# Expert inputs of a mixture-of-experts stage: rows scattered once to DRAM in slot order instead of gathered for every job

## The chip, the cores and the metric

The kernel runs on one core of one Trainium2 chip. The core has TensorE (PE for matmuls, PEld for its weight loads), VectorE (DVE), ScalarE (ACT), GpSimd (POOL) and SyncE (SP), and 16 DMA engines that all queues share. The metric is the device time of one execution in microseconds; less is better.

## The reference, cut to what matters

A two-layer decoder trunk on 256 tokens of width 1024, all in float32. Layer 0 is sparse attention and a dense SwiGLU of width 2816, layer 1 is stick-breaking attention and a top-2-of-8 expert SwiGLU. What the change touches is the last part:

```python
def moe_ffn(u, router_w, w_gate_up, w_down):
    logits = (tok @ router_w)
    top_vals, top_idx = lax.top_k(logits, 2)
    gates = jax.nn.softmax(top_vals, axis=-1)
    ...
    for e in range(8):
        y = y + dense_gates[:, e:e + 1] * swiglu(tok, w_gate_up[e], w_down[e])
```

The weights of the eight experts are 8 x (1024 x 5632 + 2816 x 1024) floats, and each is read from DRAM once.

## The kernel before, in words

The kernel is one hand-ordered program with one instruction stream for each engine and semaphores between them. Its stages are: attention of layer 0 (to about 104 us of the span), dense SwiGLU in 11 steps (about 17 us each in the middle, to 297 us), shared keys and values and layer 1's attention (to about 398 us), router and routing (to about 423 us), and then the experts.

**Jobs.** An expert gets its tokens in jobs of 96 slots. There are at least 8 jobs, one for each expert; experts with more than 96 tokens would get further ones, up to 24. Jobs 0 to 7 ran here. A job has 12 up tiles (`expert_up`, two transfers each, 2 MB a tile for the first eight and 1.5 MB for the last four) and 11 down tiles (`expert_dn`, 1 MB each). PE's order is written out in `iteration(k, i)`: up tile `i`, then down tile `i - 4`; up tiles 0 to 2 of the next job are put among the last down tiles of this one. Up tiles lie in a ring of 6, down tiles in a ring of 4, and SP refills a place in this fixed order as soon as PE has done with it. SP's transfers go through one queue (q1), those of POOL through another (q0).

**The input of a job** is `m_u`, the 96 tokens' rows transposed to 8 blocks of 128 x 96. Job 0 gets it from products of `h` with a 0/1 matrix `m_pick` on PE (`gather_first`). For job k + 1, during job k:

- DVE makes `m_pick` of the next job (`pick`, at i = 3).
- PE multiplies it with the token numbers (`slot_tokens`, at i = 5: 12 small matmuls with one column), and DVE turns the result into `slot_token`, 96 row numbers (`tokens_known`, at i = 6). A slot without a token gets row number 0.
- POOL fetches these 96 rows of `u_rows` by an indirect DMA into `m_x`, 96 partitions x 1024 (`fetch` in `save`). `u_rows` is the normalised stream, 256 x 1024, which POOL wrote to DRAM in `late_routing`'s time with two plain DMAs.
- PE transposes `m_x` in 8 pieces (`gather`, at i = 8), and DVE multiplies them with the norm's weight into `m_u` (`gathered`, at i = 9). ACT copies `m_u` to `m_u_now` between two jobs.

**The output of a job**, `m_y`, is saved by POOL to `y_rows`, a DRAM tensor of 24 x 96 rows of which rows from job 7 on are cleared beforehand: in attention of layer 0, by one DMA from a zeroed tile. After the last save, each token's two rows are gathered from `y_rows` with four indirect DMAs (`y_first`, `y_second`) while the last job runs, and the last job's own rows are added by products on PE.

**The dense stage** matters because of the clearing. Step i needs up tile i (2 MB, in runs of 1 KB) and down tile i (1 MB, in runs of 4 KB) from SP's queue. SP issues up tile i once DVE has split up tile i - 4, and right behind it down tile i - 2 once down tile i - 6 is split. ACT starts the split of a tile (`up_piece`, `dn_piece`), so an ACT row tells when a tile has to be there.

Of the kernel before, what the change touches and what calls it, by code (L numbers as in the profile page):

```python
# [44 lines left out]
NO_SLOT = -1.0e4  # L45
# [3 lines left out]
K_EPS, K_ROW, K_TOKEN = 928, 929, 945  # L49
# [7 lines left out]
T_IN, T_OUT, T_DENSE = 0, 5, 7  # L57
# [9 lines left out]
def program(nc, x, a_norm_w, a_w_in, a_q_norm_w, a_k_norm_w, a_w_out, kv_norm_w, kv_w, b_norm_w,  # L67
# [6 lines left out]
    with ctx:  # L74
        def sb(name, shape, dt=f32):
            return ctx.enter_context(nc.sbuf_tensor(name, shape, dt))

        def sem(name):
            return ctx.enter_context(nc.semaphore(name))
# [45 lines left out]
        slot_token = sb("slot_token", [SLOTS, 1], i32)  # L125
        u_rows = nc.dram_tensor("u_rows", (TOK, DM), f32, kind="Internal").ap()
# [81 lines left out]
        m_x = u[0:SLOTS, 0, :]  # L208
# [62 lines left out]
        u_ready, u_out, m_x_in, e_token_ps, e_token = (sem(n) for n in ("u_ready", "u_out", "m_x_in", "e_token_ps", "e_token"))  # L271
# [226 lines left out]
        def _(pe):  # L498
# [409 lines left out]
            def slot_tokens(j):  # L908

                pe.wait_ge(e_pick, j + 1)  # L910
                for t in range(NT):
                    for n in range(3):
                        mm = on_third(bank[4][THIRD * n:THIRD * n + THIRD, 0:1], m_pick[:, t, THIRD * n:THIRD * n + THIRD],
                                      cst[:, K_TOKEN + t:K_TOKEN + t + 1], n, t == 0, t == NT - 1)
                mm.then_inc(e_token_ps, 1)

# [10 lines left out]

            def gather(j):

                pe.wait_ge(m_x_in, 16 * j)  # L930
                for b in range(KD):
                    c = SLOTS * (b % 4)
                    mm = pe.transpose(bank[4 + b // 4][:, c:c + SLOTS], m_x[:, P * b:P * b + P], ident[0:SLOTS, 0:SLOTS])  # L933
                mm.then_inc(e_gather, 1)
# [79 lines left out]
            def iteration(k, i, last=False):  # L1014
                if i < E_UP or not last:
                    expert_up(k, i)
                if i == 5 and not last:
                    pe.wait_ge(e_u, k + 1)
                    slot_tokens(k + 1)
                if i == 8 and not last:  # L1020
                    gather(k + 1)
                if i == 6 and last:
                    pe.wait_ge(e_pick, k + 1)
                    pe.wait_ge(e_u, k + 1)
# [403 lines left out]
        def _(pool):  # L1428
# [4 lines left out]
            for j, (angle, first) in enumerate(((cos, 0), (sin, 16), (cos, 16), (sin, 0))):  # L1433
# [5 lines left out]
            pool.dma_start(y_rows[(NEXP - 1) * SLOTS:, :].rearrange("(j s) c -> s j c", s=SLOTS),  # L1439
                           m_y.unsqueeze(1).to_broadcast([SLOTS, JOBS - NEXP + 1, DM])).then_inc(y_cleared, 16)  # L1440
# [21 lines left out]
            for t in range(NT):  # L1462
                pool.wait_ge(u_ready, t + 1)
                pool.dma_start(u_rows[P * t:P * t + P, :], u[:, t, :]).then_inc(u_out, 16)
# [5 lines left out]
            pool.wait_ge(u_out, 16 * NT)  # L1470
# [14 lines left out]
            first_row, second_row, gate1, gate2 = (folded(v) for v in (first_row, second_row, gate1, gate2))  # L1485
# [9 lines left out]

            def save(k):

                pool.wait_ge(y_saved, k + 1)
                pool.wait_ge(e_gather, k + 1)
                pool.wait_ge(e_token, k + 1)  # L1500
# [16 lines left out]
            pool.wait_ge(e_gather, last_job + 1)  # L1517
# [13 lines left out]
        def _(dve):  # L1531
# [290 lines left out]
            dve.wait_ge(y_cleared, 16)  # L1822
            scaled_heads(q_T[:, 0:4, :], pair[bq_pair[0]]).then_inc(bq_sb, 1)
# [84 lines left out]
            def tokens_known(j):  # L1908
                dve.wait_ge(e_token_ps, j)
                dve.tensor_copy(slot_token[:, 0:1], bank[4][0:SLOTS, 0:1]).then_inc(e_token, 1)  # L1910

# [24 lines left out]
            def gathered(k):  # L1936
                dve.wait_ge(e_gather, k + 1)
                dve.wait_ge(e_u_now, k)
                w = nw[:, KD * NORM_F1:KD * (NORM_F1 + 1)].rearrange("p (b j) -> p b j", b=2).unsqueeze(3)\
                    .to_broadcast([P, 2, 4, SLOTS])  # L1940
                src = pair[2][:, :].rearrange("p (b c) -> p b c", b=2)[:, :, 0:4 * SLOTS].rearrange("p b (j c) -> p b j c", j=4)
                dve.tensor_tensor(m_u.rearrange("p (b j c) -> p b j c", b=2, j=4), src, w, ALU.mult).then_inc(e_u, 1)
# [29 lines left out]
            def iteration(k, i, last=False):  # L1972
                if i % 4 == 3 and i < E_UP:
                    hidden_step(k, i // 4)
                if i == STEPS - 1 + E_DN_LATE:
                    result(k)
                if i == 3 and not last:
                    dve.wait_ge(e_gather, k + 1)
                    pick(k + 1)
                if i == 6 and not last:  # L1980
                    tokens_known(k + 1)
# [11 lines left out]
            def late_routing():  # L1993
                for t in range(NT):
                    dve.tensor_scalar(u[:, t, :], h[:, t, :], rs[:, 3, t:t + 1], None, ALU.mult).then_inc(u_ready, 1)
# [3 lines left out]
                for t in range(NT):  # L1999
                    dve.tensor_tensor_scan(rows_f[:, 1, t, :], ones[:, 0:NEXP], routed[:, t, :], 0.0, ALU.mult, ALU.add)  # L2000
# [63 lines left out]
```

## Time and profile before

| what | value |
| --- | --- |
| median of 3 runs | 1129.88 us (1128.78 to 1129.98) |
| the profiled execution | 1128.54 us, its span 1126.7 us |
| granted clock of TensorE | 1.0 |
| PE busy | 1113.7 us, 99% of the span |
| DMA moved | 361.30 MB, mean 321 GB/s |
| one job (up tile 8 to up tile 8) | 86.5 us |

In the 40 slices of the span PE is busy in all of them. The DMA row has gaps up to the 14th slice and is at 9 tenths from then until the last two; the rate is near 411 GB/s in most of those slices.

### The profile page before, as it was taken

How to read it: one execution, taken by the hardware profiler on the slowest of the kernel's cores; microseconds unless marked ns; L12 is line 12 of the kernel's file. 1: busy time of each engine (PE TensorE's matmuls, PEld its weight loads, DVE VectorE, ACT ScalarE, POOL GpSimd, SP SyncE). 2: the span in 40 equal slices, each digit the busy share in tenths (PEclk: the TensorE clock that was granted, in tenths of full speed). 3: DMA queues.
4: the chain of work that ended last, by engine and by line, in shares of the span. 5: the costliest groups of instructions: out<-in, count | busy, mean ns of one | idle time of the engine just before them, and what ended most of it. 6: DMA issues, size and time to landing. Idle time of an engine off the chain costs nothing.

```text
span 1126.7 us, 32768 instructions
## 1 busy us (share of the span) xinstructions
PE 1113.7 (99%) x15160; PEld 893.7 (79%) x15160; DVE 304.8 (27%) x466; ACT 254.9 (23%) x384; POOL 30.5 (3%) x84
## 2 busy tenths in 40 slices
PE   9999999999999999999999999999999999999998
PEld 7768999999899876678778778778778778878765
DVE  3785645545664342001001010010010010110021
ACT  4775534434547531000000000000001000000000
POOL 0000000000000002000000000000000000000100
PEclk9999999999999999999999999999999999999999
DMA  9639976454144289999999999999999999999983
GB/s 337 214 126 295 335 272 214 160 187 150 57 168 150 75 346 399 363 412 409 397 411 411 396 411 411 392 411 410 398 411 411 383 411 410 385 411 391 410 357 128
DMA packets 114214, 361.30 MB, mean 321 GB/s; under 512 B 6872, under 2 KB 33920, under 8 KB 102816
## 3 DMA queue, kind: packets, MB, share of 16 engines
q1 hardware_dynamic: 109776, 343.78, 79.0%
q0 software_dynamic: 4080, 15.34, 4.0%
q8 instruction: 121, 1.98, 0.7%
q10 hardware_dynamic: 224, 0.09, 0.0%
q14 instruction: 13, 0.11, 0.0%
HBM read 347.65 MB, written 11.53 MB: 319 GB/s over the span
## 4 chain that ended last, share of the span: by engine, by line
PE 91%; DMA 4%; DVE 2%; ACT 1%; SPq 0%; issue 0%; ACTq 0%; DVEq 0%
PE pair L938 57%; PE pair L519 9%; PE pair L520 9%; PE pair L521 9%; DMA dn_ring<-in_moe_w_down 4%; PE pair L555 1%; PE pair L581 1%; PE pair L933 1%; PE pair L536 0%; DVE up_lo L1566 0%; PE pair L620 0%; DVE dn_ring L1671 0%; PE pair L923 0%; ACT up_hi L1075 0%; PE pair L857 0%
## 5 line engine op out<-in xcount | busy, mean ns | idle before, releaser
L938 PE MATMUL pair<-up_ring,work 128*32 128x256 f32 (+1 forms) x6144 | 323.9, 366 | 0.0
L938 PEld LDWEIGHTS pair<-up_ring,work 128*32 128x32 f32 x6144 | 239.0, 110 | 73.6
L938 PE MATMUL pair<-dn_ring,e_mem 128*32 128x256 f32 (+1 forms) x3168 | 245.7, 450 | 1.9 <-DMA dn_ring<-in_moe_w_down 1.7
L938 PEld LDWEIGHTS pair<-dn_ring,e_mem 128*32 128x32 f32 x3168 | 147.6, 110 | 76.9 <-DMA dn_ring<-in_moe_w_down 3.5
L938 PE MATMUL pair<-up_more,work 128*32 128x192 f32 (+1 forms) x3072 | 152.5, 352 | 0.0
L938 PEld LDWEIGHTS pair<-up_more,work 128*32 128x32 f32 x3072 | 133.2, 110 | 13.8
L519 PE MATMUL pair<-uT_hi,up_hi 128*128 128x256 f32 x480 | 135.5, 282 | 0.8 <-DVE uT_lo L1580 0.6
L1566 DVE TENSOR_TENSOR up_lo<-up_ring,up_hi 128x2048 fp32r<-128x2048 f32 x46 | 105.3, 2291 | 112.4 <-ACT up_hi L1075 112.3
L520 PE MATMUL pair<-uT_lo,up_hi 128*128 128x256 f32 x480 | 134.8, 281 | 0.0
L521 PE MATMUL pair<-uT_hi,up_lo 128*128 128x256 f32 x480 | 134.8, 281 | 0.0
L1390 ACT ACTIVATE e_mem<-pair 128x768 f32<-128x768 f32 (+1 forms) x24 | 18.2, 758 | 479.3 <-PE pair L938 479.3
L1961 DVE TENSOR_TENSOR e_mem<-e_mem,pair 128x768 f32<-128x768 f32 (+1 forms) x24 | 21.3, 888 | 333.9 <-PE pair L938 333.9
L1075 ACT ACTIVATE up_hi<-up_ring 128x2048 fp32r<-128x2048 f32 x46 | 87.9, 1913 | 101.5 <-PE pair L521 97.0
L519 PEld LDWEIGHTS pair<-uT_hi,up_hi 128*128 128x128 f32 x480 | 90.4, 188 | 2.1 <-issue 1.3
L520 PEld LDWEIGHTS pair<-uT_lo,up_hi 128*128 128x128 f32 x480 | 90.4, 188 | 0.4
L521 PEld LDWEIGHTS pair<-uT_hi,up_lo 128*128 128x128 f32 x480 | 90.4, 188 | 0.0
L519 PE MATMUL pair<-up_hi,uT_hi 128*128 128x512 f32 x128 | 51.7, 404 | 1.1 <-DVE uT_lo L1590 1.1
L1969 DVE COPY q_T<-pair 96x256 f32<-96x256 f32 x8 | 3.4, 420 | 179.2 <-PE pair L938 179.2
L520 PE MATMUL pair<-up_lo,uT_hi 128*128 128x512 f32 x128 | 50.6, 395 | 0.0
L521 PE MATMUL pair<-up_hi,uT_lo 128*128 128x512 f32 x128 | 50.5, 395 | 0.0
L1075 ACT ACTIVATE q_T<-pair 32x256 f32<-32x256 f32 (+2 forms) x30 | 14.3, 480 | 90.7 <-PE pair L938 82.1
L520 PE MATMUL pair<-dn_lo,hid_hi 128*128 128x512 f32 x80 | 31.6, 395 | 0.0
(299 smaller groups left out, 778.0 us busy)
## 6 DMA issues: line engine op xcount, KB each, us to landing
up_ring<-in_moe_w_gate_up SPq DMA_DIRECT2D x96, 1024.0 KB, 10.3
dn_ring<-in_moe_w_down SPq DMA_DIRECT2D x88, 1024.0 KB, 16.8
up_more<-in_moe_w_gate_up SPq DMA_DIRECT2D x32, 1024.0 KB, 12.9
up_ring<-in_moe_w_gate_up SPq DMA_DIRECT2D x32, 768.0 KB, 10.8
up_more<-in_moe_w_gate_up SPq DMA_DIRECT2D x32, 768.0 KB, 10.6
up_ring<-in_dense_w_gate_up SPq DMA_DIRECT2D x22, 1024.0 KB, 9.0
dn_ring<-in_dense_w_down SPq DMA_DIRECT2D x11, 1024.0 KB, 11.1
up_ring<-in_kv_w SPq DMA_DIRECT2D x4, 2048.0 KB, 7.9
```

What stands on the lines that cost most here:

```text
L519: pe.matmul(ps, a_hi, b_hi, start=start, stop=False, skip_group_check=shared)
L520: pe.matmul(ps, a_hi, b_lo, start=False, stop=False, skip_group_check=shared)
L521: return pe.matmul(ps, a_lo, b_hi, start=False, stop=stop, skip_group_check=shared)
L555: mm = pe.matmul(bank[2 * t + g][:, 0:I_HALF], uT_in[:, k, P * t:P * t + P], index_tile(half)[:, j, I_HALF * g:I_HALF * g + I_HALF], start ...
L581: mm = pe.matmul(bank[(NT * j + t) % 4][:, 0:cols], uT_in[:, k, P * t:P * t + P], up_tile(j, cols)[:, k, :], start=(k == 0), stop=(k == KD ...
L933: mm = pe.transpose(bank[4 + b // 4][:, c:c + SLOTS], m_x[:, P * b:P * b + P], ident[0:SLOTS, 0:SLOTS])
L938: return pe.matmul(out, a, w, start=start, stop=stop, tile_position=(0, THIRD * place), skip_group_check=True)
L1075: return act.activation(out_, in_, ACT.Copy, scale=scale)
L1390: act.activation(m_hid[:, 0:3 * cols].rearrange("p (n c) -> p n c", n=3), gate_ps[:, 0:768].rearrange("p (n c) -> p n c", n=3)[:, :, 0:col ...
L1566: dve.tensor_tensor(buffer(up_lo, n, 2048), raw_piece(n), buffer(up_hi, n, 2048).bitcast(f32), ALU.subtract).then_inc(up_l, 1 + unsplit)
L1961: dve.tensor_tensor(v, v, up_ps[:, 0:768].rearrange("p (n c) -> p n c", n=3)[:, :, 0:cols], ALU.mult).then_inc(e_raw, 1)
L1969: dve.tensor_copy(m_y[:, 512:768], bank[3][0:SLOTS, 0:256])
```

## The change

`u_rows` goes. In its place stands `x_rows`, 24 x 96 rows in slot order, of which the rows of jobs 1 to 23 are cleared with two DMAs. The clearing of `y_rows` moves from the first attention into the dense stage, in front of them. Once the slot rows are computed, POOL scatters the 256 rows of `u` into `x_rows` with four indirect DMAs (first choice and second choice of each token). In the jobs a fetch is four plain DMAs of 32 partitions x 3 x 256, whose place depends on the job number alone. `u` is written with its columns permuted so that 32 x 32 blocks come together, DVE transposes the fetched tile (128 x 768) by blocks into `m_xT`, and `gathered` reads that. `slot_tokens`, `gather`, `tokens_known` and the `pick` of jobs 1 to 6 go. DVE waits for the clearing before it reuses `q_T`.

```diff
+        rows_x = sb("rows_x", [P, 2, NT], i32)
+        x_rows = nc.dram_tensor("x_rows", (JOBS * SLOTS, DM), f32, kind="Internal").ap()
...
-        m_x = u[0:SLOTS, 0, :]
+        m_x = u[:, 0, 0:768]
+        m_xT = e_mem[:, 768 + GROUPS * 768:2 * 768 + GROUPS * 768]
...
-                if i == 5 and not last:
-                    pe.wait_ge(e_u, k + 1)
-                    slot_tokens(k + 1)
-                if i == 8 and not last:
-                    gather(k + 1)
...
+            pool.wait_ge(up_used, 2 * (T_DENSE + 3))
+            def clear(rows, first, end, done):
+                pool.dma_start(rows[first * SLOTS:end * SLOTS, :].rearrange("(j s) c -> s j c", s=SLOTS),
+                               m_y.unsqueeze(1).to_broadcast([SLOTS, end - first, DM])).then_inc(done, 16)
+            clear(y_rows, NEXP - 1, JOBS, y_cleared)
+            clear(x_rows, 1, 12, x_cleared)
+            clear(x_rows, 12, JOBS, x_cleared)
...
             def fetch(j):
-                pool.indirect_dma_start(m_x, None, u_rows, bass.IndirectOffsetOnAxis(slot_token[:, 0:1], 0)).then_inc(m_x_in, 16)
+                for place in range(4):
+                    part = slice(THIRD * place, THIRD * place + THIRD)
+                    src = x_rows[bass.ds(j * SLOTS, SLOTS), 256 * place:256 * place + 256]
+                    pool.dma_start(m_x[part, :].rearrange("t (n c) -> t n c", n=3),
+                                   src.rearrange("(n t) c -> t n c", n=3)).then_inc(m_x_in, 16)
...
+            pool.wait_ge(u_ready, NT)
+            pool.wait_ge(x_cleared, 32)
+            for which in range(2):
+                for t in range(NT):
+                    pool.indirect_dma_start(x_rows, bass.IndirectOffsetOnAxis(rows_x[:, which, t:t + 1], 0), u[:, t, :], None)\
+                        .then_inc(x_out, 16)
...
             def gathered(k):
-                dve.wait_ge(e_gather, k + 1)
+                dve.wait_ge(m_x_in, 64 * k)
+                dve.transpose(m_xT.rearrange("p (b t) -> p b t", t=THIRD), m_x.rearrange("p (b c) -> p b c", c=THIRD))\
+                   .then_inc(x_free, 1)
```

## Rows read from the trace of the kernel before

**Rows 1.** The page's slices: busy tenths, then GB/s of all DMA queues together.

```profile
PE   9999999999999999999999999999999999999998
DMA  9639976454144289999999999999999999999983
GB/s 337 214 126 295 335 272 214 160 187 150 57 168 150 75 346 399 363 412 409 397 411 411 396 411 411 392 411 410 398 411 411 383 411 410 385 411 391 410 357 128
```

**Rows 2.** Waits of PE: line waited for, us in total, times, longest.

```profile
PE pair L938 <- DMA dn_ring<-in_moe_w_down: 1.7, 1, 1.7
```

**Rows 3.** Windows: us, PE, PEld, DVE, ACT, POOL busy (instructions); PEclk, DMA share, GB/s.

```profile
452.00:538.00 86.00, 86.00 (x1567) 65.18 (x1563) 7.69 (x12) 4.67 (x8) 2.01 (x4) 1.00 1.01 398
...
971.00:1037.00 66.00, 66.00 (x1220) 49.17 (x1213) 4.62 (x6) 3.12 (x4) 1.14 (x2) 1.00 1.00 393
```

**Rows 4.** DMA issues in 480:509, 683:712, 1000:1029: xcount, KB, median us to landing.

```profile
dn_ring<-in_moe_w_down SPq DMA_DIRECT2D x3, 1024.0 KB, 10.8
...
dn_ring<-in_moe_w_down SPq DMA_DIRECT2D x4, 1024.0 KB, 15.3
...
dn_ring<-in_moe_w_down SPq DMA_DIRECT2D x3, 1024.0 KB, 21.5
```

**Rows 5.** Chain that ended last, its end: start, us, what.

```profile
1065.55 22.12 DMA dn_ring<-in_moe_w_down
...
1087.71 30.08 PE pair L938 x456
```

**Rows 6.** Timeline of PE in job 2: start, us, instructions; slot products, then transposes.

```profile
630.31 0.27 PE L938 MATMUL pair<-cst,work 128*32 128x1 f32 x11
...
652.55 0.88 PE L933 MATMUL pair<-cst,u 96*128 96x96 f32 x8
```

**Rows 7.** Windows of 6 us: at `u_rows`' write, a save, three fetches, `y_first`'s gather.

```profile
428.00:434.00 6.00, 6.00 (x116) 3.66 (x112) 0.00 (x0) 0.00 (x0) 0.00 (x0) 1.00 1.02 404
...
532.00:538.00 6.00, 6.00 (x107) 5.32 (x103) 1.44 (x4) 0.00 (x0) 0.18 (x1) 1.00 1.03 413
...
635.00:641.00 6.00, 6.00 (x106) 3.60 (x102) 0.00 (x0) 0.00 (x0) 0.00 (x0) 1.00 1.03 349
...
463.00:469.00 6.00, 6.00 (x107) 3.61 (x100) 0.00 (x0) 0.00 (x0) 0.00 (x0) 1.00 1.03 338
...
808.00:814.00 6.00, 6.00 (x108) 3.62 (x104) 0.00 (x0) 0.00 (x0) 0.00 (x0) 1.00 1.03 357
...
1061.00:1067.00 6.00, 5.95 (x104) 3.53 (x97) 0.00 (x0) 0.81 (x1) 0.00 (x0) 1.00 1.04 413
```

**Rows 8.** DMA in 120:150, the dense loads alone.

```profile
DMA packets 7781, 10.23 MB, mean 341 GB/s; under 512 B 152, under 2 KB 7003, under 8 KB 7778
```

**Rows 9.** Timeline of POOL: end of job 0's save; timeline of DVE: second hidden step, job 1.

```profile
535.74 0.18 POOL L1508 TENSOR_TENSOR tick<-tick 1x1 f32<-1x1 f32 x1 [7.09 <-DMA y_rows<-q_T]
...
560.71 0.98 DVE L1963 STREAM_TRANSPOSE e_mem<-e_mem 128x768 f32<-128x768 f32 x1
```

**Rows 10.** DMA issues in 60:120, then the queues in 96:102 (packets, MB, share).

```profile
y_rows<-q_T POOLq DMA_DIRECT2D x1, 6528.0 KB, 33.5
...
q0 software_dynamic: 400, 1.63, 86.6%
q1 hardware_dynamic: 301, 0.31, 14.4%
```

**Rows 11.** Timelines of SP and ACT in the dense stage, from 149 us.

```profile
154.02 0.99 SPq L423 DMA_DIRECT2D up_ring<-in_dense_w_gate_up  x2
...
170.98 0.99 SPq L423 DMA_DIRECT2D up_ring<-in_dense_w_gate_up  x2
...
149.75 1.92 ACT L1075 ACTIVATE up_hi<-up_ring 128x2048 fp32r<-128x2048 f32 x1 [3.71 <-PE pair L521]
...
206.04 1.04 ACT L1075 ACTIVATE dn_hi<-dn_ring 128x1024 fp32r<-128x1024 f32 x1
...
223.00 1.05 ACT L1075 ACTIVATE dn_hi<-dn_ring 128x1024 fp32r<-128x1024 f32 x1
```

More of the change, by code:

```diff
@@ L270, in program @@
         row_step = sem("row_step")
-        u_ready, u_out, m_x_in, e_token_ps, e_token = (sem(n) for n in ("u_ready", "u_out", "m_x_in", "e_token_ps", "e_token"))
+        u_ready, x_cleared, x_out, m_x_in, x_free = (sem(n) for n in ("u_ready", "x_cleared", "x_out", "m_x_in", "x_free"))
         block = ctx.enter_context(nc.Block())
@@ L905, in _ @@
             keep_clock(1)
[L908 to L915, printed above, removed]
             def gather_first():
@@ L926, in gather_first @@
                         mm.then_inc(first_gather if k < KD - 1 else e_gather, 1)
[L928 to L934, printed above, removed]
             def on_third(out, a, w, place, start, stop):
@@ L1484, in _ @@
             then_next(pool.tensor_tensor(gate2, gate, second, ALU.mult))
-            first_row, second_row, gate1, gate2 = (folded(v) for v in (first_row, second_row, gate1, gate2))
+            first_row, second_row = (folded(v) for v in (first_row, second_row))
+            then_next(pool.tensor_scalar(rows_x[:, 0, :].unsqueeze(2), first_row, NO_SLOT, None, ALU.add))
+            then_next(pool.tensor_scalar(rows_x[:, 1, :].unsqueeze(2), second_row, NO_SLOT, None, ALU.add))
+            pool.wait_ge(u_ready, NT)
[4 more added lines that the diff above has]
+                        .then_inc(x_out, 16)
+            gate1, gate2 = (folded(v) for v in (gate1, gate2))
             then_next(pool.tensor_scalar(spare[:, 0, 0:1], misc[:, 0, 6:7], float(SLOTS), float((NEXP - 1) * SLOTS) - NO_SLOT,
@@ L1494, in _ @@
             then_next(pool.tensor_scalar(rows_i[:, 1, :].unsqueeze(2), second_row, NO_SLOT, None, ALU.add))
+            pool.wait_ge(x_out, 16 * 2 * NT)
             def save(k):
                 pool.wait_ge(y_saved, k + 1)
-                pool.wait_ge(e_gather, k + 1)
-                pool.wait_ge(e_token, k + 1)
+                pool.wait_ge(x_free, k + 1)
                 pool.tensor_tensor(tick, tick, tick, ALU.mult).then_inc(tick_done, 1)
@@ L1516, in _ @@
             pool.wait_ge(y_saved, last_job + 1)
-            pool.wait_ge(e_gather, last_job + 1)
+            pool.wait_ge(x_free, last_job + 1)
             pool.tensor_tensor(tick, tick, tick, ALU.mult).then_inc(tick_last, 1)
@@ L1822, in _ @@
             dve.wait_ge(y_cleared, 16)
+            dve.wait_ge(x_cleared, 32)
             scaled_heads(q_T[:, 0:4, :], pair[bq_pair[0]]).then_inc(bq_sb, 1)
@@ L1936, in gathered @@
             def gathered(k):
-                dve.wait_ge(e_gather, k + 1)
+                dve.wait_ge(m_x_in, 64 * k)
+                dve.transpose(m_xT.rearrange("p (b t) -> p b t", t=THIRD), m_x.rearrange("p (b c) -> p b c", c=THIRD))\
+                   .then_inc(x_free, 1)
+                dve.wait_ge(x_free, k + 1)
                 dve.wait_ge(e_u_now, k)
[L1939 to L1942, printed above, removed]
+                w = nw[:, KD * NORM_F1:KD * (NORM_F1 + 1)].unsqueeze(1).unsqueeze(3).to_broadcast([P, 3, KD, THIRD])
+                dve.tensor_tensor(m_u.rearrange("p (k n t) -> p n k t", n=3, t=THIRD),
+                                  m_xT.rearrange("p (n k t) -> p n k t", n=3, t=THIRD), w, ALU.mult).then_inc(e_u, 1)
             def add_saved(rows_in, rows, which, t):
@@ L1976, in iteration @@
                     result(k)
[L1977 to L1981, printed above, removed]
+                if i == 3 and last:
+                    dve.wait_ge(e_gather, 1)
+                    pick(k)
                 if i == 9 and not last:
@@ L1994, in late_routing @@
                 for t in range(NT):
-                    dve.tensor_scalar(u[:, t, :], h[:, t, :], rs[:, 3, t:t + 1], None, ALU.mult).then_inc(u_ready, 1)
+                    dve.tensor_scalar(u[:, t, :].rearrange("p (q k c) -> p k q c", q=4, c=THIRD),
+                                      h[:, t, :].rearrange("p (k q c) -> p k q c", q=4, c=THIRD),
+                                      rs[:, 3, t:t + 1], None, ALU.mult).then_inc(u_ready, 1)
                 dve.wait_ge(first_u_dve, 2)
@@ L1999, in late_routing @@
                 for t in range(NT):
-                    dve.tensor_tensor_scan(rows_f[:, 1, t, :], ones[:, 0:NEXP], routed[:, t, :], 0.0, ALU.mult, ALU.add)
+                    last = dve.tensor_tensor_scan(rows_f[:, 1, t, :], ones[:, 0:NEXP], routed[:, t, :], 0.0, ALU.mult, ALU.add)
+                last.then_inc(x_free, 1)
                 dve.tensor_scalar(n_last_job[:, :], misc[:, 0, 6:7], float(NEXP - 1), None, ALU.add).then_inc(e_u, 1)
```

14 lines of the change are left out of this document (1 added, 13 removed).

## The prediction, made before the changed kernel ran

> **What bounds the kernel now.** I read the slices of the page first. PE is busy in every slice, which invites the sum "what leaves PE is gained". But the DMA row stands at 9 from the 15th slice to the last two, which is the whole expert stage, at rates near 411 GB/s [rows 1]. Two resources are full there, and the question is which one sets the end.
>
> PE's waits say "not DMA", at first sight: in the whole run PE waited for a transfer once, 1.7 us [rows 2]. The windows say more: the DMA share is 1.00 to 1.01 in the first job as in the last [rows 3]. So the engines always have work queued. The issues show the queue growing: a down tile lands 10.8 us after its issue in job 1, 15.3 us in job 3 and 21.5 us in job 7 [rows 4]. DMA is slower than PE by a little in each job, and PE lives on what was loaded before it began. The last rows of the chain show that reserve used up: a down tile issued at 1065.55 lands 22.12 us later, PE waits for it, and from 1087.71 on 30.08 us of PE work run to the last job's products [rows 5]. So the end is: when DMA has worked through everything ahead of that tile, plus a fixed tail. I therefore count DMA time, and PE time only as a second limit.
>
> **What PE loses.** In each of seven jobs the transposes go, 0.81 us (0.88 with the end of the last; the next group starts 0.81 later), and the slot products. Those start at 630.31 and hold the down tile back by some 0.13 us. Together 0.94 us, times 7, is 6.6 us [rows 6]. If PE alone set the end, its wait would go too: 6.6 + 1.7 = 8.3 us at most. By the reading above none of this arrives at the end. PE only comes earlier to the tile that it waits for.
>
> **What DMA loses: seven gathers.** A gather moves 96 x 4 KB = 0.39 MB. At 410 GB/s that is 0.96 us. But it also slows what runs beside it: the 6 us around a fetch move 349 GB/s (338 to 357 in the seven of them), where 6 us around a save of the same size move 413 [rows 7]. At a mean of 347 the loss is 63 GB/s x 6 us = 0.38 MB, or 0.92 us. A gather costs 1.88 us. Why the dip? Not because it is indirect: `y_first`'s gather, 1.05 MB of it, leaves 413 GB/s in its window [rows 7]. What is different is that a slot without a token asks for row 0. 512 choices on 8 x 96 slots leave one slot in three empty, some 32 reads of one 4 KB row at once. I take this as the cause. In `x_rows` every slot has its own row, so the dip should go.
>
> **What DMA gains: seven plain fetches.** The same 0.39 MB in 384 runs of 1 KB. The nearest rows are the dense loads, which are mostly of 1 KB runs and move 341 GB/s with DMA full [rows 8]: 0.39 / 0.341 = 1.15 us. Ends: 0.95 us (the save's 413 GB/s) and 2.07 us (1.15 with the dip of 0.92 kept). I take 1.15, since it is the rate of the same run length. Saved: 1.88 - 1.15 = 0.73 us a job, 5.1 us over seven; the ends give 6.5 us saved and 1.3 us lost.
>
> The Trainium skill, "DMA: Bandwidth & Descriptors", Specifications, has 512 B as the least transfer that still runs at line rate. By that rule the fetch of 1 KB runs would cost no more than 4 KB runs, the 0.95 us end. The 341 GB/s of the dense loads against 411 speak for a price, and the row decides.
>
> **What DMA gains: the scatter.** `u_rows` was written with 1.05 MB, `x_rows` with two rows for each token, 2.1 MB. The window of the old write moved 404 GB/s, so 1.05 MB cost 2.6 us, and as much again is added [rows 7]. DMA is full from 397 us on, so nothing hides it: +2.6 us (2.0 if it goes at the 410 to 413 of the other windows less what overlaps, 3.8 if it makes a dip like the gathers').
>
> **Sum for DMA:** -5.1 + 2.6 = -2.5 us; ends -6.5 + 2.0 = -4.5 and +1.3 + 3.8 = +5.1.
>
> **What costs nothing, and its cover.**
> - The first fetch: `x_out` is complete some 15 us after the routing's 427 us plus 10 us of row arithmetic, near 455, the fetch near 470, and job 1's first tile wants `m_u` near 502. If this cover went, PE would wait at each job's start.
> - Later fetches: job 0's save is done at 535.74, so fetch 2 lands before 548 (a fetch took 9 us). DVE asks for it behind the second hidden step, 560.71 [rows 9]. 12 us of cover. Behind the waiting DVE instruction stands the third hidden step, at which PE's down tiles 8 to 10 hang.
> - DVE's added block transpose is 0.98 us by the hidden step's of the same shape [rows 9], and `u`'s permuted write may take 1.4 us more in all; DVE works 8 us in 86 [rows 3]. The `pick`s that go give half of it back.
> - POOL issues four DMAs instead of one, some 2 to 3 us in a job in which it works 2 us of 86 [rows 3].
> - DVE's new wait for the clearing stands at about 318 us, long after its end.
>
> **The clearing** is the step I trust least. Before, 6.68 MB went at 81.8 us; now 15.7 MB go from 149.75 us, which is when `up_used` reaches 20 (ACT's split waits for the same count) [rows 11]. In a window inside the old clearing q0 took 86.6% of 6 us for 1.63 MB [rows 10], so 15.7 MB need 50 us of all 16 engines. Beside it run the dense loads, 3.15 MB a step, 9.2 us at 341 GB/s. Down tile 5, issued behind the up tile of 154.02, is split at 206.04; down tile 6, issued behind that of 170.98, at 223.00 [rows 11]. All the work up to down tile 6 is 50 + 2 x 9.2 = 68 us and ends at 218, 5 us before it is wanted. If the clearing went first, down tile 5 would land at 149.8 + 50 + 9 = 209, 3 us late. I take 0, with little cover, and see it as a rival.
>
> **From the sum to the time.** The profiled execution took 1128.54 us, its span and 1.84 us around it: 1126.0 us after. The median of the runs shown is 1.34 us above it, so 1129.88 - 2.5 = 1127.4 us. A measurement of this kernel tells about 0.2%, 2.3 us, from no change; the forecast lies on that edge.
>
> **The rivals.**
> - *PE sets the end.* For it: one wait of 1.7 us in the whole run [rows 2], and PE at 9 tenths throughout. Against it: the landing times that double [rows 4]. It gives -6.6 us, 1123.3 us; 1121.6 with the wait gone.
> - *The clearing holds up the dense stage (slower side).* The place is down tile 5 or 6, and it decides once the clearing and the loads together need more than the 73 us from 149.75 to 223.0. For it: in 96:102 the clearing moved 1.63 MB in 400 packets and the loads 0.31 MB in 301, though SP was issuing behind them [rows 10]. They take turns by packet, and a load's packet has a quarter of the bytes. Also, the old clearing took 33.5 us to land where its engine time is 21: some engines are slower. At that ratio 50 us become 79, and the tile is up to 24 us late. Against it: the rings hold three steps. I price it at 5 us, -2.5 + 5: 1132.4 us. The page named above, Queues, rings and completion order, has an engine serving its queues in turns by packet. By that rule it is the 1 KB loads that give way, as the row shows.
> - *The fetch is no cheaper.* The dip comes from POOL's writing into the tile and not from repeated rows: 2.07 us against 1.88, +1.3 + 2.6: 1133.8 us.
> - *The savings and the scatter cancel*: a shorter dip than I took, or a scatter with a dip: within 1 us of before, 1129.5 us.
>
> **Chances.** Forecast 0.40, PE sets the end 0.17, clearing 0.20, fetch no cheaper 0.09, cancelling 0.14. The forecast's own range is 1125.5 to 1129.0, half of it below the line of 0.2% (1127.6). Faster: 0.22 + 0.17 + 0.05 = 0.44 (the last where the clearing costs little). Same: 0.18 + 0.14 + 0.03 = 0.35. Slower: 0.12 + 0.09 = 0.21. Range: from the PE rival, 1122.5, up to 1132.5, which leaves out the dearer half of the clearing and the dear fetch, and the last us of PE's case.
>
> **What would show it.** The windows around a fetch at 380 to 413 GB/s instead of 347; the period of a job 0.94 us shorter while the DMA share stays at 1.0; landing times that grow at least as fast as before; more wait of PE for `dn_ring` in jobs 6 and 7, 5 to 7 us instead of 1.7; the tail of 30 us unchanged. I am wrong if PE's waits stay at 2 us or less while the time falls by 6 us (PE bounds), if PE waits near 206 or 223 us (the clearing), or if the fetch windows stay near 350 (the dip's cause).

## The result, and the profile after

The changed kernel takes 1136.53 us (median of 4 runs, 1135.36 to 1137.37). The kernel before took 1129.33 us in the 4 runs compared with them. The ratio is 1.0060, 95% interval 1.0048 to 1.0072: it is slower, by 6.8 us or 0.6% (5.4 to 8.1 us). The forecast was 1127.4 us, and the result lies 4.0 us above the range, which ended at 1132.5.

Page of the changed kernel: busy time by engine, the slices, the DMA queues of software, and the costliest group of PE in the expert stage's second half.

```profile
PE 1111.8 (98%) x15020; PEld 866.5 (76%) x15020; DVE 307.6 (27%) x454; ACT 254.6 (22%) x384; POOL 44.5 (4%) x111
...
PE   9999999999999999999999999999999999899998
...
DMA  9636789796144299999999999999999999999993
GB/s 335 211 118 223 257 269 335 249 356 240 64 159 149 74 363 379 384 412 411 384 412 411 387 412 412 390 412 412 367 412 411 383 411 407 377 412 390 410 361 124
...
q0 software_dynamic: 7168, 25.43, 6.8%
...
L922 PE MATMUL pair<-dn_ring,e_mem 128*32 128x256 f32 (+1 forms) x3168 | 268.9, 450 | 10.9 <-DMA dn_ring<-in_moe_w_down 10.7
```

The slices of the expert stage look almost as before [rows 1]: DMA is full from the 15th on. What is new stands at the end of the last row: PE waits 10.7 us for down tiles, in eleven waits, where it waited once for 1.7 us [rows 2]. L922 after is the line L938 of before.

Waits of PE, whole run, changed kernel (us in total, times, longest).

```profile
PE pair L922 <- DMA dn_ring<-in_moe_w_down: 10.7, 11, 2.2
...
PE pair L520 <- DVE hid_lo L1791: 1.1, 1, 1.1
```

DMA issues of the changed kernel in 480:509, 683:712 and 1000:1029 (count, KB, median us to landing).

```profile
dn_ring<-in_moe_w_down SPq DMA_DIRECT2D x4, 1024.0 KB, 12.0
...
dn_ring<-in_moe_w_down SPq DMA_DIRECT2D x4, 1024.0 KB, 21.8
...
dn_ring<-in_moe_w_down SPq DMA_DIRECT2D x5, 1024.0 KB, 21.2
```

Before, these were 10.8, 15.3 and 21.5 [rows 4]. So 21 to 22 us seems to be the most that the rings allow. The old kernel came to it in the last job, the new one in job 3. The length of a job says the same. Between two copies of `m_u` on ACT lie 86.49 us in the kernel before, six times. In the changed kernel it is 85.53 us three times, 0.96 less, as predicted, and then 88.1, 89.0 and 89.5 us. So the reserve is used up in job 3, and from job 4 on a us that DMA needs is a us of the span. The tail is the old one to 0.04 us [rows 5].

The end of the chain that ended last, changed kernel (start, us, what).

```profile
1050.55 21.35 DMA dn_ring<-in_moe_w_down
1071.94 2.38 PE pair L922 x17
1074.31 22.21 DMA dn_ring<-in_moe_w_down
1096.56 30.04 PE pair L922 x456
```

Windows of the changed kernel: two jobs; the scatter; fetches 1, 2 and 7; a stretch after fetch 2; a save (columns as in [rows 3]).

```profile
452.00:538.00 86.00, 86.00 (x1567) 66.83 (x1561) 8.06 (x10) 4.67 (x8) 3.09 (x6) 1.00 1.02 402
971.00:1037.00 66.00, 62.67 (x1144) 45.77 (x1140) 5.28 (x6) 2.31 (x3) 2.59 (x6) 1.00 1.02 398
...
439.00:452.00 13.00, 12.37 (x210) 8.81 (x211) 1.93 (x2) 0.00 (x0) 4.21 (x16) 1.00 1.02 398
...
456.00:464.00 8.00, 8.00 (x144) 5.78 (x140) 0.00 (x0) 0.81 (x1) 0.00 (x0) 1.00 1.05 318
543.00:551.00 8.00, 8.00 (x144) 7.04 (x140) 0.00 (x0) 0.81 (x1) 0.00 (x0) 1.00 1.03 321
978.00:986.00 8.00, 6.06 (x110) 3.60 (x106) 0.00 (x0) 0.81 (x1) 0.00 (x0) 1.00 1.00 317
...
552.00:560.00 8.00, 8.00 (x144) 7.33 (x139) 0.00 (x0) 0.00 (x0) 0.00 (x0) 1.00 1.03 409
...
705.00:711.00 6.00, 6.00 (x110) 3.41 (x106) 1.93 (x2) 0.00 (x0) 1.15 (x4) 1.00 1.03 420
```

A fetch is now spread over some 8 us, so its window is 8 us. The seven windows moved 318, 321, 328, 345, 332, 332 and 317 GB/s, a mean of 327.6, and the stretch behind moves 409. The dip did not go. It costs 8 x (410 - 327.6) / 410 = 1.61 us, and 0.96 for the bytes: 2.57 us a fetch, where a gather cost 1.88.

In the dense stage, the chain of the changed kernel in 205:240, then ACT's splits of down tiles.

```profile
189.44 21.07 SPq L424
210.56 22.53 DMA dn_ring<-in_dense_w_down
233.11 1.07 ACT dn_hi L1053
...
214.23 1.06 ACT L1053 ACTIVATE dn_hi<-dn_ring 128x1024 fp32r<-128x1024 f32 x1 [7.52 <-DMA dn_ring<-in_dense_w_down]
...
233.11 1.06 ACT L1053 ACTIVATE dn_hi<-dn_ring 128x1024 fp32r<-128x1024 f32 x1 [8.74 <-DMA dn_ring<-in_dense_w_down]
```

Down tiles 5 and 6 were split at 206.04 and 223.00 [rows 11]. They are now split at 214.23 and 233.11, 8 and 10 us late, beside the larger clearing. PE lost little of it: its first expert matmul starts at 425.60 instead of 423.72, 1.9 us later. And 0.6 of these 1.9 us were there before the clearing began: ACT's second splits of down tile 4 start at 191.12 and 190.55, and the two traces are already 0.6 us apart at 36 us, where nothing was changed. The clearing cost 1.3 us, of which 1.1 is PE's wait for `hid_lo`.

| Part | Working | us |
|---|---|---|
| Ahead of the clearing, where nothing was changed | there at 36 us in these two executions | +0.6 |
| Dense stage, beside the clearing | 425.60 - 423.72 - 0.6 | +1.3 |
| Scatter, 2.10 MB for 1.05 | the window moved 398 GB/s, the old one 404 | +2.6 |
| Seven fetches | 7 x (2.57 - 1.88) | +4.8 |
| Sum | | +9.3 |
| Measured | spans of the profiled runs 1135.5 - 1126.7 | +8.8 |

The medians differ by less, 6.8 to 7.2 us. Against them the ledger is some 2 us too dear, 0.6 of it the start of these two executions. No run here measured the scatter by itself.

### The profile page after: what moved, and what is told of

Read it like the earlier page. It is cut to its first block, busy times and chain, and to the rows that moved or that the text cites. A ratio compares the mean times of both kernels' runs of the same rounds, so it can differ in the third digit from the quotient of the medians.

```text
span 1135.5 us, 32543 instructions
## 1 busy us (share of the span) xinstructions
PE 1111.8 (98%) x15020; PEld 866.5 (76%) x15020; DVE 307.6 (27%) x454; ACT 254.6 (22%) x384; POOL 44.5 (4%) x111
## 4 chain that ended last, share of the span: by engine, by line
PE 68%; DMA 14%; SPq 12%; DVE 3%; ACT 2%; issue 1%; ACTq 0%; DVEq 0%
PE pair L922 39%; DMA dn_ring<-in_moe_w_down 12%; PE pair L520 8%; PE pair L522 7%; PE pair L521 7%; SPq L447 6%; SPq L453 4%; DMA dn_ring<-in_dense_w_down 2%; SPq L424 2%; PE pair L556 1%; PE pair L582 1%; DVE up_lo L1561 1%; ACT up_hi L1053 0%; PE pair L537 0%; PE pair L621 0%
## 5 line engine op out<-in xcount | busy, mean ns | idle before, releaser
L922 PE MATMUL pair<-up_ring,work 128*32 128x256 f32 (+1 forms) x6144 | 343.0, 366 | 0.6 <-issue 0.3
L922 PEld LDWEIGHTS pair<-up_ring,work 128*32 128x32 f32 x6144 | 242.6, 110 | 80.8 <-issue 2.7
L922 PE MATMUL pair<-dn_ring,e_mem 128*32 128x256 f32 (+1 forms) x3168 | 268.9, 450 | 10.9 <-DMA dn_ring<-in_moe_w_down 10.7
L922 PEld LDWEIGHTS pair<-dn_ring,e_mem 128*32 128x32 f32 x3168 | 151.2, 110 | 92.5 <-DMA dn_ring<-in_moe_w_down 16.8
L922 PE MATMUL pair<-up_more,work 128*32 128x192 f32 (+1 forms) x3072 | 161.2, 353 | 0.0
L922 PEld LDWEIGHTS pair<-up_more,work 128*32 128x32 f32 x3072 | 123.5, 110 | 28.4
L1566 DVE TENSOR_TENSOR dn_lo<-dn_ring,dn_hi 128x1024 fp32r<-128x1024 f32 x22 | 26.9, 1223 | 21.9 <-ACT dn_hi L1053 21.9
```

Source lines behind the costliest of these rows:

```text
L1566: dve.tensor_tensor(buffer(dn_lo, n, DM), ffn_dn((n // 2) % RING)[:, n % 2, :], buffer(dn_hi, n, DM).bitcast(f32), ALU.subtract).then_inc( ...
```

## The experiments

Four questions: is it the fetches, and what in them; is it the clearing; is DMA the bound and not PE; is there a version that keeps the gain. Each kernel was timed against the kernel before on the same chip. On those chips the kernel before took 1129.3 to 1130.4 us, so differences between two experiments are taken from their ratios.

**1. One fetch of 4 KB rows onto 96 partitions** (changed kernel, DVE waits for 16 instead of 64).

```diff
-                for place in range(4):
...
+                pool.dma_start(u[0:SLOTS, 0, :], x_rows[bass.ds(j * SLOTS, SLOTS), :]).then_inc(m_x_in, 16)
```

> The changed kernel with each job's fetch as one plain DMA of 96 rows of 4 KB onto 96 partitions instead of four DMAs of 1 KB pieces; the rows then do not lie as the block transpose wants them, so jobs 1 to 7 compute on wrong inputs. In the changed kernel the 8 us around a fetch move 328 GB/s (mean of seven) where 409 is usual: 1.6 us of DMA lost beside the 0.96 us of its own bytes. Theory shape (the form of the fetch costs it: 1 KB pieces or 32 partitions at a time): the windows rise to 400 or more and the time falls by 7 x 1.6 = 11 us, as long as DMA stays the bound, to about 1126. Rival source (reading a fresh, small DRAM region through POOL's queue costs it, in any form): windows stay at 330 to 350, time stays within 2 us of the changed kernel, 1134 to 1137.

Measured: 1133.74 us, ratio 1.0028 (1.0018 to 1.0037). Fetch windows of 6 us, the first two of this kernel:

```profile
541.00:547.00 6.00, 6.00 (x107) 5.13 (x102) 0.00 (x0) 0.81 (x1) 0.00 (x0) 1.00 1.02 350
626.00:632.00 6.00, 6.00 (x107) 3.89 (x103) 0.00 (x0) 0.81 (x1) 0.00 (x0) 1.00 1.02 324
```

It is cheaper than the four fetches, but the dip is that of the gathers [rows 7]. These are plain reads of distinct rows of 4 KB. So the dip is not of indirection, not of repeated rows, and not of short runs alone.

**2. One fetch of 1 KB runs onto 128 partitions** (changed kernel).

```diff
-                for place in range(4):
...
+                src = x_rows[bass.ds(j * SLOTS, SLOTS), :].rearrange("(n t) (q c) -> (t q) n c", n=3, q=4)
+                pool.dma_start(m_x.rearrange("p (n c) -> p n c", n=3), src).then_inc(m_x_in, 16)
```

> The changed kernel with the fetch as one plain DMA onto all 128 partitions, still in 384 pieces of 1 KB (partition 4t+q instead of 32q+t, so jobs 1 to 7 compute on wrong inputs). Rival within the theory shape: if it is the 32 partitions at a time, windows rise to 400 and the time falls by some 11 us, to about 1126; if it is the 1 KB pieces, windows stay near 330 and the time near 1136.

Measured: 1127.61 us, ratio 0.9976 (0.9967 to 0.9986), 9.5 us under the changed kernel. The same two windows:

```profile
541.00:547.00 6.00, 6.00 (x106) 5.11 (x101) 0.00 (x0) 0.81 (x1) 0.00 (x0) 1.00 1.02 396
626.00:632.00 6.00, 6.00 (x107) 3.91 (x103) 0.00 (x0) 0.81 (x1) 0.00 (x0) 1.00 1.02 395
...
PE pair L922 <- DMA dn_ring<-in_moe_w_down: 4.9, 7, 1.5
```

The bytes and the 1 KB runs are the changed kernel's; the dip is nearly gone (377 to 396 GB/s in jobs 1 to 4; 367 and 355 in jobs 5 and 6). What remains different is that one DMA writes 128 partitions, instead of four that write 32 each.

**3. The gather of the kernel before, each slot from a row of its own.**

```diff
-                dve.tensor_copy(slot_token[:, 0:1], bank[4][0:SLOTS, 0:1]).then_inc(e_token, 1)
+                dve.tensor_copy(slot_token[:, 0:1], cst[0:SLOTS, K_TOKEN:K_TOKEN + 1]).then_inc(e_token, 1)
```

> The kernel before with its indirect gather, but slot s always fetches row s of u_rows, so no row is asked for twice (jobs 1 to 7 compute on wrong inputs); slot products and transposes on PE stay. The prediction's cause (some 32 reads of row 0): the 6 us windows around a gather rise from 347 GB/s to 400 or more. Rival: they stay at 340 to 357, and the repeated row was not the cause. The time can fall by 2 us at most, PE's waits, since PE bounds right behind them.

Measured, one run: 1130.19 us, as before. Two of its fetch windows:

```profile
549.00:555.00 6.00, 6.00 (x108) 3.59 (x104) 0.00 (x0) 0.00 (x0) 0.00 (x0) 1.00 1.04 349
636.00:642.00 6.00, 6.00 (x108) 3.59 (x100) 0.00 (x0) 0.00 (x0) 0.00 (x0) 1.00 1.02 347
```

No row is read twice in one gather, and the dip is the same. The cause that the prediction took is refuted.

**4. One small clearing of jobs 1 to 7 at its old place, 82 us** (changed kernel; 9.4 MB are cleared there).

```diff
-            pool.wait_ge(up_used, 2 * (T_DENSE + 3))
...
-            clear(x_rows, 1, 12, x_cleared)
-            clear(x_rows, 12, JOBS, x_cleared)
+            clear(x_rows, 1, NEXP, x_cleared)
```

> The changed kernel with y_rows cleared where it was before and of x_rows only the rows of jobs 1 to 7, there too (2.8 MB instead of 9.0). Theory: the clearing in the dense stage costs the 1.85 us by which the changed kernel is late at its end, so the time falls by about 2 us, to 1134.5, and PE waits nowhere in the dense stage. Rival: the clearing costs nothing, all 7 us and more arise in the jobs: no change within 1 us.

Measured: 1141.34 us, ratio 1.0095 (1.0074 to 1.0115): some 4 us slower than the changed kernel, though 6.3 MB less are cleared. PE's wait in the dense stage, and a window there, this kernel:

```profile
PE pair L520 <- DVE hid_lo L1788: 3.6, 1, 3.6
...
104.00:150.00 46.00, 42.29 (x298) 39.41 (x297) 28.23 (x33) 22.35 (x29) 0.00 (x0) 0.93 0.90 300
```

The old place took 6.68 MB without a wait of PE there, and it has no room for 9.4 MB. The wait is only part of the price. PE, busy throughout before, stands still from 132.3 to 135.9 us. Its granted clock then is at 0.50, the lower of its two levels (1.2 GHz), from 136 to 142, and full again from 143 on. Six us at half the clock lose some 3 us. At the end of the dense stage this kernel is 6.2 us behind the kernel before.

**5. All clearing later, from about 235 us** (changed kernel).

```diff
-            pool.wait_ge(up_used, 2 * (T_DENSE + 3))
+            pool.wait_ge(up_used, 2 * (T_DENSE + 8))
```

> The changed kernel with all three clearings begun five dense steps later (up_used 30 instead of 20, about 235 us instead of 150), when the dense loads are all issued and the DMA moves 76 to 202 GB/s. In the changed kernel the expert stage begins 1.8 us late and PE waits 1.1 us for the down tile's split at 223. Theory: that is the clearing's price; the time falls by 1.8 us against the changed kernel, to about 1134.8, unless the layer 1 loads at 255 to 273 are now the late ones. Rival: the clearing costs the same wherever it stands, 1136.5.

Measured: 1143.88 us, ratio 1.0122 (1.0105 to 1.0139), 7.0 us slower than the changed kernel. Waits of this kernel:

```profile
PE pair L520 <- DVE up_lo L1561: 4.8, 2, 4.5
...
DVE q_T L1812 <- DMA x_rows<-q_T: 5.9, 1, 5.9
```

The dense stage now loses nothing, but the next layer's weights and the reuse of `q_T` come late: PE's first expert matmul starts at 431.7 us, 8.1 later than before the change.

**6. The fetch cut to 16 pieces of 512 B** (changed kernel).

```diff
-                for place in range(4):
...
+                pool.dma_start(m_x[0:16, 0:128], x_rows[bass.ds(j * SLOTS, 16), 0:128]).then_inc(m_x_in, 16)
```

> The changed kernel with each fetch cut to 16 pieces of 512 B (jobs 1 to 7 then compute on stale inputs). By the windows a fetch costs 0.96 + 1.6 = 2.6 us of DMA, 18 us in seven. Theory DMA bound: the time falls until PE bounds, which is the kernel before less 6.6 us for the products and 1.7 us of waits, plus 1.8 us of the clearing: 1122.8 to 1124, with PE's waits for down tiles near 0. Rival (fetches are not what costs; the DMA work of the expert stage grew otherwise): less than 5 us gained, above 1131.

Measured: 1123.52 us, ratio 0.9939 (0.9922 to 0.9955). PE no longer waits for a down tile. By the ratios the seven fetches were worth 13.7 us. By 2.57 us each they would be 18; PE stops the gain. So PE's bound lies near 1123.5 us. The prediction's PE rival gave 1121.6 us with the waits gone, and with the 1.9 us by which the expert stage starts later that is 1123.5. That its other number, 1123.3, is as close is luck: it kept a wait and knew of no delay.

**7. The kernel before with one of eight transposes and one of twelve slot products left in each job.** Its gather brings the fixed rows of experiment 3.

```diff
-                for t in range(NT):
-                    for n in range(3):
+                for t in range(NT - 1, NT):
+                    for n in range(2, 3):
...
-                for b in range(KD):
+                for b in range(1):
```

> The kernel before with the indirect gather kept (distinct constant rows), but one transpose of eight and one slot product of twelve on PE in each job (jobs 1 to 7 compute on wrong inputs): some 0.8 us a job less on PE, 5.6 us in seven. Theory DMA bound: PE only waits more for down tiles (1.7 us before, some 6 to 7 us now), the time stays within 1 us of the kernel before. Rival PE bound: the time falls by 4 us or more, to 1125 or less.

Measured: 1128.79 us, ratio 0.9990 (0.9980 to 0.9999). PE's wait in it:

```profile
PE pair L938 <- DMA dn_ring<-in_moe_w_down: 4.9, 6, 1.4
```

A job is 0.59 us shorter on PE (85.90 us), 4 us in seven. Of this 0.1%, 1 us, reaches the time. The rest comes back as wait, 4.9 us for 1.7 [rows 2].

**8. Pieces of 1 KB scattered so that one load onto 128 partitions brings a job's rows in the right order**, with the clearing of experiment 5. It computes the reference.

```diff
+                    for q in range(4):
+                        pool.indirect_dma_start(x_rows, bass.IndirectOffsetOnAxis(rows_x[:, which, q, t:t + 1], 0),
+                                                u[:, t, 256 * q:256 * q + 256], None).then_inc(x_out, 16)
```

> A version that computes the reference: the changed kernel with x_rows laid out in pieces of 256, so that a fetch is one plain DMA onto 128 partitions of 3 KB each; the scatter becomes 16 indirect DMAs of 128 pieces of 1 KB instead of 4 of 4 KB rows, with some 8 us more of row arithmetic on POOL; clearing as in a_clear_late. Theory partitions (a load onto all 128 partitions makes no dip): fetch windows at 400 GB/s or more; against a_wide's 1127.6 it gains the 1.8 us of the clearing and loses about 1 us to the smaller scatter pieces: 1126 to 1127.5, faster than the kernel before. Rival: the scatter of 1 KB pieces makes a dip of its own, or the first fetch comes too late for job 1: 1129 or more.

Measured: 1150.54 us, ratio 1.0181 (1.0164 to 1.0198). First a window of job 1, then one at the scatter, then POOL's scatter instructions, then PE's matmuls and waits there:

```profile
538.00:625.00 87.00, 87.00 (x1583) 76.76 (x1579) 8.07 (x10) 4.66 (x8) 1.53 (x4) 1.00 1.02 410
...
452.00:480.00 28.00, 20.59 (x143) 7.89 (x145) 1.93 (x2) 0.00 (x0) 17.68 (x36) 0.70 0.51 169
...
451.28 0.96 POOL L1486 DMA_INDIRECT x_rows<-u,rows_x  x1 [0.30 <-issue]
...
454.34 0.62 PE L923 MATMUL pair<-up_more,work 128*32 128x256 f32 x4 [0.34 <-issue]
...
PEld pair L923 <- issue: 19.5, 31, 1.9
```

The fetch part does what was hoped: a whole job with its fetch in it runs at 410 GB/s. Two things eat it. The late clearing costs about what it cost in experiment 5: the first expert matmul starts at 430.7 us (431.7 there, 423.7 before). And while POOL issues sixteen scatters, from 448.6 to 468.7 us, PE is busy for only 20.6 of 28 us, with DMA half idle. The 0.70 is a mean of the two levels: the granted clock is full until 458, in spite of PE's gaps from 454 on, and at 0.50 from 461 to 476. Job 0 takes some 19 us longer than in the kernel before. Why PE issues slowly there was not settled.

**9. The kernel before, gathered in three indirect DMAs of 1 KB pieces onto 128 partitions, and transposed on DVE.** No scatter and no clearing. It computes the reference.

```diff
-                pool.indirect_dma_start(m_x, None, u_rows, bass.IndirectOffsetOnAxis(slot_token[:, 0:1], 0)).then_inc(m_x_in, 16)
+                for n in range(3):
+                    pool.indirect_dma_start(m_x[:, 256 * n:256 * n + 256], None, u_rows,
+                                            bass.IndirectOffsetOnAxis(slot_token[:, n:n + 1], 0)).then_inc(m_x_in, 16)
```

> A version that computes the reference and has neither scatter nor clearing of x_rows: the kernel before, with u_rows laid out in pieces of 256 (row = 256 q + token), fetched in each job by three indirect DMAs of 128 pieces of 1 KB onto all 128 partitions, then transposed on DVE as in the changed kernel. PE keeps slot products, 48 tiny matmul passes instead of 12 (about 0.4 us a job more), and loses the 0.81 us of transposes. Theory partitions: fetch windows near 400 GB/s instead of 347, 0.85 us of DMA a job or 6 us saved; PE saves 7 x 0.4 = 3 us and its 1.7 us of waits: 1124.5 to 1126, faster than the kernel before by 0.3 to 0.45%. Rival: indirect DMAs of 1 KB pieces make the dip themselves, or three indirect DMAs hold up PE's instructions as sixteen did in v_pieces: 1130 or more.

Measured: 1124.98 us (1124.14 to 1125.39), ratio 0.9958 (0.9944 to 0.9972). Two fetch windows and PE's wait:

```profile
549.00:555.00 6.00, 6.00 (x107) 4.56 (x100) 0.00 (x0) 0.00 (x0) 0.00 (x0) 1.00 1.03 389
635.00:641.00 6.00, 6.00 (x105) 4.59 (x100) 0.00 (x0) 0.00 (x0) 0.00 (x0) 1.00 1.02 396
...
PE pair L943 <- DMA dn_ring<-in_moe_w_down: 2.2, 3, 1.5
```

It beats both kernels. Indirect loads onto 128 partitions make hardly a dip, so the indirection is cleared from this side too. Nor is it the number of DMAs: here three follow one another without the dip, and in experiment 1 a single one made it. The gain needs both resources: a job on PE is 0.54 us shorter (85.95 us, 3.8 in seven), and the cheaper fetch lets it arrive.

**10. `y_rows` cleared at 82 us as before, only `x_rows` (9.0 MB) in the dense stage** (changed kernel).

```diff
+            clear(y_rows, NEXP - 1, JOBS, y_cleared)
             pool.wait_ge(up_used, 2 * (T_DENSE + 3))
...
-            clear(y_rows, NEXP - 1, JOBS, y_cleared)
```

> The changed kernel with y_rows cleared at 82 us as before and x_rows alone (9.0 MB) in the dense stage, at the place of the change. a_clear_7 cleared 9.4 MB at 82 us and lost 3.6 us more in the dense stage than the changed kernel, a_clear_late lost 7 us in layer 1. Theory: only the amount beside the dense loads decides; 29 us of engine time instead of 50 leaves 20 us of slack at down tile 6, so the 1.8 us go: 1134.7. Rival: any clearing there costs it: 1136.5.

Measured: 1134.91 us, ratio 1.0051 (1.0035 to 1.0066), 1.0 us under the changed kernel by the ratios, but the two intervals overlap. The trace is clearer: the wait for `hid_lo` is gone, the dense stage takes what it took before to 0.1 us, and the first expert matmul starts at 423.6 us. At the later place 9.0 MB beside the dense loads cost nothing that shows and 15.7 MB 1.3 us; at the old place 6.68 MB cost no wait and 9.4 MB 3.6 us of it. So at both places the amount beside the loads decides.

**11. Experiment 2 as two DMAs onto 64 partitions each.**

```diff
+                for half in range(2):
+                    part = slice(64 * half, 64 * half + 64)
+                    pool.dma_start(m_x[part, :].rearrange("p (n c) -> p n c", n=3), src[part, :, :]).then_inc(m_x_in, 16)
```

> As a_wide, but the fetch is two DMAs of 64 partitions instead of one of 128 (jobs 1 to 7 compute on wrong inputs). Bytes, 1 KB pieces and source are the same. If the number of partitions of a DMA decides, its windows lie between a_wide's (near 400 GB/s) and the changed kernel's (328 over 8 us) and PE waits more than in a_wide; if not, they are as a_wide's.

Measured, one run: 1136.56 us, PE's wait 11.4 us. Its first two fetch windows:

```profile
540.00:546.00 6.00, 6.00 (x105) 5.14 (x101) 0.00 (x0) 0.81 (x1) 0.00 (x0) 1.00 1.03 280
625.00:631.00 6.00, 6.00 (x107) 3.92 (x103) 0.00 (x0) 0.81 (x1) 0.00 (x0) 1.00 1.03 323
```

The same runs to the same places, in two halves, and all of experiment 2's gain is gone.

**12. The kernel before, its gather widened from 96 to 128 rows and partitions.** The 32 added rows are row 0 again and nobody reads them. It computes the reference.

```diff
-        slot_token = sb("slot_token", [SLOTS, 1], i32)
+        slot_token = sb("slot_token", [P, 1], i32)
...
-        m_x = u[0:SLOTS, 0, :]
+        m_x = u[:, 0, :]
...
+            dve.memset(slot_token[:, :], 0)
```

> A version that computes the reference: the kernel before, its indirect gather widened from 96 to 128 rows of 4 KB (the last 32 ask for row 0 and are not used), so that it goes onto all 128 partitions. A third more bytes, 0.52 MB or 1.28 us. If the number of partitions decides for an indirect gather of whole rows too, the 6 us windows around it rise from 347 to 400 GB/s or more although 32 rows and more are asked for repeatedly, and a gather costs 1.3 us instead of 1.9; the time falls by about PE's 1.7 us of waits, 1127.5 to 1128.5. If repeated rows or indirect 4 KB rows matter, windows stay near 350 and the time rises by some 2 us.

Measured: 1126.06 us (1124.68 to 1126.39), ratio 0.9964 (0.9953 to 0.9976). Two fetch windows and PE's wait:

```profile
549.00:555.00 6.00, 6.00 (x104) 3.59 (x100) 0.00 (x0) 0.00 (x0) 0.00 (x0) 1.00 1.03 406
635.00:641.00 6.00, 6.00 (x108) 3.62 (x100) 0.00 (x0) 0.00 (x0) 0.00 (x0) 1.00 1.03 402
...
PE pair L938 <- DMA dn_ring<-in_moe_w_down: 0.2, 1, 0.2
```

A third more bytes, 32 more requests for one row, and yet the dip is gone and the kernel 4.1 us faster: for the cause of the dip this is the cleanest proof. The size of the gain is not explained. At most 2 us were expected, since PE stood only 1.7 us in the trace before, and in the two traces this kernel wins 2.0 us in the last job. Before that PE keeps the same 86.49 us a job. Of the 4.0 us between the two spans, 0.5 arises before the experts and 1.4 behind PE's last matmul, where the two kernels do the same. Part of the rest may be that the trace before shows a fast execution: 1128.54 us, where the median here was 1130.41. Experiments 9 and 12 can't be told apart in time, since their intervals overlap. Both beat both kernels.

The experiments in one table. The cost of a fetch is its bytes at 410 GB/s and the loss in its window, 6 x (410 - rate) / 410 (8 us for the changed kernel), at the mean of the windows read.

| Fetch | Partitions of one DMA | Windows, GB/s | 16 us from the issue, GB/s | One fetch, us | Kernel, us |
|---|---|---|---|---|---|
| Before, indirect, 4 KB | 96 | 338 to 357 | 384 | 1.88 | 1129.33 |
| 3, distinct rows | 96 | 313 to 349 | 382 | 2.01 | 1130.19 |
| 12, widened | 128 | 378 to 406 | 404 | 1.46 | 1126.06 |
| 9, indirect, 1 KB | 128 | 389 to 397 | 400 | 1.19 | 1124.98 |
| Changed, plain, 1 KB | 32 | 317 to 345 | 366 | 2.57 | 1136.53 |
| 11, plain, 1 KB | 64 | 280 to 323 | 359 | 2.50 | 1136.56 |
| 1, plain, 4 KB | 96 | 317 to 364 | 376 | 2.00 | 1133.74 |
| 2, plain, 1 KB | 128 | 377 to 396 | 397 | 1.24 | 1127.61 |

The fourth column is the mean of fetches 2 to 7 in windows of 16 us that begin with POOL's issue. The loss is in these too, in nearly the same order, so the short windows do not make it by where they lie. The short windows of the experiments are mostly of jobs 1 to 4. In jobs 5 and 6 the loads onto 128 partitions lose somewhat more.

Seven times a difference in the fifth column can be held against the times, here by the ratios: from the changed kernel to experiment 2 it is 7 x 1.33 = 9.3 us for 9.5 measured; to experiment 1, 7 x 0.57 = 4.0 for 3.6. From before to 9 it is 7 x 0.69 = 4.8 for 4.7, though there PE's shorter job had to allow it. For 12 it gives 2.9, and 4.1 were measured, so 1.2 us of that gain have no row.

## Why the prediction was wrong

- *DMA sets the end, not PE: right.* The landing times at their ceiling from job 3 on, the unchanged tail, and experiments 6 and 7 from both sides show it. PE's saving of 6.6 us went into waits. In the kernel before DMA held PE up only in the last job, for some 2 us, so PE was close behind as a bound. That part of the argument also says that each us added to DMA arrives in full, which is what happened.
- *A gather costs 1.88 us, of it 0.92 a dip: right as a row of the windows.* The time of experiment 12 seems to confirm it: it takes the dip away and pays 0.32 us for its 0.13 MB of added rows, 7 x (0.92 - 0.32) = 4.2 us, and 4.1 were measured. That is in part luck. Its windows keep 0.18 us of the dip, which makes it 2.9, and in the traces only 2.0 us arise in the jobs.
- *The cause of the dip, and the plain fetch at 1.15 us: the step that failed.* "What is different is that a slot without a token asks for row 0" named one difference out of several. The comparison was with a save, and with `y_first`'s gather. Both also differ in what this kernel's gathers alone do: they load onto 96 partitions. `y_first`'s rows go onto all 128, and the save reads SBUF and does not write it. Experiments 3 and 12 rule the repeated row out. Experiments 2 and 11 show the number of partitions with the same runs, and experiments 1 and 9 rule out the number of DMAs, the one other thing in which these two differ. The change splits the load of 96 partitions into four of 32, and so made the dip dearer: 2.57 us instead of 1.15. That is 7 x 1.42 = 9.9 us on a forecast that missed by 9.1 (with the clearing's 1.3 it is too much by the same 2 us as the ledger).
- *Runs of 1 KB are dear, by the dense loads' 341 GB/s: the row did not fit the case.* Experiments 2 and 9 fetch 1 KB runs, and their windows move 377 to 397 GB/s. But in the trace the fetch of experiment 2 is 112 packets for 0.39 MB, and no packet of 512 B to 2 KB stands in its 16 us, while 7003 of the dense loads' 7781 packets are under 2 KB [rows 8]. So these fetches are not packets of 1 KB, and whether such packets are dear no run settles.
- *The scatter +2.6 us: right as far as the ledger shows.* It made no dip like a fetch's (398 GB/s).
- *The clearing at nothing: wrong by 1.3 us.* The rival had the right place (down tiles 5 and 6), and what the trace shows fits its mechanism, turns by packet. It also had the length nearly right, 79 us: the slower of the two clearings of `x_rows` landed 74.4 us after its issue. In 160:180 q0 moved 5.34 MB in 1316 packets and the loads 1.28 MB in 1263, and a down tile took 56.6 us to land. The rival's 5 us were too many, since the rings hid most of it: tiles 8 and 10 us late cost PE 1.3.
- *The covers of the fetch and DVE's added transpose: right.* PE waits for no `m_u`; its only new waits are for `dn_ring` and the 1.1 us at `hid_lo`.

No rival was right alone. "The fetch is no cheaper" (+1.3 us for the fetches, 1133.8) had the right sign and too small a size, and its reason, that POOL's queue writes into the tile, falls with experiments 2 and 12, whose loads come from that queue too. With the clearing's 1.3 us it comes to 1135.1, 1.4 below what was measured. The two were given chances as if only one could hold.

What in the chip makes fewer partitions dear was not measured. It is not that DMA engines stand idle: in the windows of the fetches the DMA share stays at 1.0, while they move up to a third less. A rule bears on it. The Trainium skill, "SBUF — State Buffer", Door 1: The DMA port swizzle, says that DMA bandwidth depends on how many of SBUF's 16 ports the partitions reach, and that partitions 0 to 63 reach no more of them than 0 to 31. By that rule loads onto 32 and onto 64 are equally bad, a load onto 96 puts two thirds of its bytes on half of the ports, and one onto 128 is even. The table agrees in its order (2.57 and 2.50, then 2.00 and 1.88, then 1.24). It does not explain why a save from 96 partitions leaves 413 GB/s [rows 7], and no trace here shows a port.

## What to carry to other kernels

Where the DMA share stands at 1.0 and the time from issue to landing grows from stage to stage, DMA sets the end however busy PE looks, and a small transfer must be priced with what it does to the large ones beside it. Let one load write all 128 partitions, even with rows that nobody needs. Splitting it by partitions, to have its rows in the right order, cost 1.3 us a load here. Before a dip is put down to one difference, list all differences between the transfers with and without it, and test the cheapest on the chip.

## What the runs showed of the hardware

- A load of 0.39 MB by four DMAs onto 32 partitions each, two onto 64 or one onto 96 costs the loads beside it 0.9 to 1.6 us; onto 128 partitions 0.2 to 0.3 us, as the mean of the windows in the table (up to 0.8 in job 6 of experiment 2). This holds for plain and indirect DMAs and for runs of 1 and 4 KB.
- A queue with 4 KB packets beside one with mostly 1 KB packets took 4 times its bytes (5.34 and 1.28 MB in 20 us) at nearly equal counts of packets.
- While POOL issued indirect scatters, one in 1.27 us, PE issued one to seven matmuls and then stood 0.3 to 0.9 us, again and again, waiting for nothing that the trace shows (experiment 8). Beside the changed kernel's four scatters it stood so once, for 0.34 us. The cause is open.
- After PE stood still for 3.6 us, its granted clock was at 0.50 (1.2 GHz) for the next 6 us and then at 1.00 again (experiment 4).
